# A hybrid encoder layer in fp32: GpSimd takes both halves of the weights that return from DRAM, values stand nine steps behind, linear attention's points are merged

## The chip, the cores and the metric

One core of a Trainium2 chip runs the whole layer. Its engines work side by side, each through its own list of instructions in order, and wait for each other by semaphores: TensorE (PE, matmuls), VectorE (DVE), ScalarE (ACT), GpSimd (POOL) and SyncE (SP), which here only starts DMAs. ScalarE starts DMAs too. The metric is the device time of one execution in microseconds (us); lower is better.

## What is computed

Two sequences of 1024 and 512 tokens of width 1024 go through one layer: RMSNorm, one input projection, three mixers, their gates, the output projection, the residual and a last RMSNorm. Cut to what the change touches:

```python
h = rmsnorm(x, norm_g); z = h @ w_in                      # one projection for all groups
# group A, latent attention, 4 heads
s = einsum(q_nope, k_nope) + einsum(q_rope, k_rope)
p = softmax(s * MLA_SCALE); o = einsum(p, v)
# group C, gated linear attention in chunks of 64, both directions summed
a = einsum('bhid,bhijd,bhjd->bhij', qc, decay, kc)        # inside a chunk
o = o_inter + einsum('bhij,bhje->bhie', a, vc)            # plus the state before the chunk
o = rmsnorm(o_f + o_b, gla_norm_g)
y = rmsnorm(x + concat(gated groups) @ w_out)
```

## The kernel before

The 1536 tokens are 12 tiles of 128 rows. Products that need fp32 are made of three fp32r matmuls: both factors are split into a high part (the value cast to fp32r) and a low part (value minus high), and `product` (L76 to L80) adds high*high, high*low and low*high.

**Front and linear attention.** `phase_front` computes the input projection in 54 blocks of 24 matmuls (128x128 by 512 columns), blocks `i` from 6 on in a plain loop, each in two halves. Between the halves other work is put in. `gla_point(i, half)` numbers the half blocks from block 21 on: p = 0, 1, 2, ... Every tile t of linear attention has three of these points, p = 3t to 3t + 2. At p = 3t TensorE runs `compare(t)`, 56 small matmuls (32 rows by 64 columns) that give all levels of the scores inside the chunks. ScalarE's `copy_top` and VectorE's `choose` (six masked copies, L1076) make the matrix `g_attn` of it. At p = 3t + 2 TensorE runs `turn_rows(t - 2)`, two 128x128 transposes (L1416), and `output(t)`: 16 matmuls of the state (L1398) and 8 of 64x64 with `g_attn` (L1404). ScalarE's `take_rows(t)` fetches the rows and squares them (L681, L685), VectorE's `sum_rows(t)` adds the squares, GpSimd's `invert_rows(t)` takes the inverse root, VectorE's `scale_rows(t)` (L1091) scales the rows in its next tile, and `turn_rows` turns them. `take_outputs` copies four turned tiles at once. ScalarE's list calls this work through `follow(p)`. GpSimd splits the projection's weights (`split_lo`, L805) between these things, in a fixed order.

**Latent attention.** `phase_mla_attend` runs 48 steps m, one per head and tile of queries. The first 8 tiles of a head have 1024 keys, the last 4 have 512. A step: TensorE computes the scores (`scores(m)`, 5 matmuls of 512 columns for every 512 keys); VectorE takes the maximum of a row (`a_top`) and the bias; ScalarE the exponential into `a_weights` (`exponentials`, L1982). In the first three heads (steps 0 to 35) the weights are turned through DRAM: VectorE transposes 32x32 blocks into one of two buffers (`a_weights` slot 2 and `a_spread_second`, L2055), ScalarE starts the store (`store_spread`), and SP, when both tiles of a pair p are stored, starts four loads that bring the pair back turned into `a_turned_lo`, one of three slots (`a_turned_lo`, `_second`, `_third`). ScalarE's `take_high(m)` then casts the loaded values into `a_turned_hi` (L2000), at step m + 5 of its own list, and GpSimd subtracts it in place (L1895). `values(p)` on TensorE (24 or 12 matmuls of 256 columns) needs both. In head 3 TensorE turns the weights itself.

At which step values, the output product (`output(p)`) and the fetch of its result (`gather(p)`) of pair p stand, on all engines, is written in three tuples, `VALUES_AT`, `OUTPUT_AT` and `GATHER_AT`. Before, `values(p)` stood at step 2p + 8 for the first 16 pairs, its output two steps later. Each engine's list is this order written out; there is no scheduler.

## Time and profile before

| | us |
|---|---|
| median of 3 runs | 747.58 |
| the runs | 745.91 to 748.26 |
| the profiled execution, its own time | 750.29 |
| its span in the profile | 748.5 |
| input projection and linear attention | up to 398 |
| latent attention | 398 to 612 |
| output projection, final norm | 612 to 748.5 |

The profile lists for each engine when each instruction started and how long it took. "PE" rows are matmuls and "PEld" rows weight loads. In a timeline the bracket behind a row is the time that the engine stood idle before it and what ended that. The granted clock of TensorE is a share of 2.4 GHz: 1.00 is 2.4, 0.50 is 1.2 GHz.

### The profile page before, as it was taken

How to read it: one execution, taken by the hardware profiler on the slowest of the kernel's cores; microseconds unless marked ns; L12 is line 12 of the kernel's file. 1: busy time of each engine (PE TensorE's matmuls, PEld its weight loads, DVE VectorE, ACT ScalarE, POOL GpSimd, SP SyncE). 2: the span in 40 equal slices, each digit the busy share in tenths (PEclk: the TensorE clock that was granted, in tenths of full speed). 3: DMA queues.
4: the chain of work that ended last, by engine and by line, in shares of the span. 5: the costliest groups of instructions: out<-in, count | busy, mean ns of one | idle time of the engine just before them, and what ended most of it. 6: DMA issues, size and time to landing. Idle time of an engine off the chain costs nothing.

```text
span 748.5 us, 14234 instructions
## 1 busy us (share of the span) xinstructions
PE 721.3 (96%) x5784; PEld 606.4 (81%) x5784; DVE 408.9 (55%) x718; ACT 311.9 (42%) x520; POOL 287.6 (38%) x290
## 2 busy tenths in 40 slices
PE   8999999999999999999999789889989999999996
PEld 6998878878888888888888588788788988888885
DVE  5855877376575543026175757758656654333232
ACT  6554444334423432233223545555554654232321
POOL 3223226366556512122400255553555854322320
PEclk9999999999999999999999889999999999999999
DMA  7613021001122233230235886786886035564441
GB/s 255 183 26 89 28 97 57 30 31 40 63 72 87 73 114 107 92 88 26 63 144 180 249 240 207 230 225 184 264 233 194 1 109 180 176 196 158 139 151 56
DMA packets 65389, 96.14 MB, mean 128 GB/s; under 512 B 6161, under 2 KB 43537, under 8 KB 65330
## 3 DMA queue, kind: packets, MB, share of 16 engines
q1 hardware_dynamic: 53856, 65.34, 30.3%
q10 hardware_dynamic: 11474, 29.96, 10.6%
q8 instruction: 43, 0.70, 0.4%
q14 instruction: 16, 0.13, 0.1%
HBM read 59.30 MB, written 35.00 MB: 126 GB/s over the span
## 4 chain that ended last, share of the span: by engine, by line
PE 76%; DVE 8%; DMA 7%; ACT 4%; POOL 2%; issue 2%; SPq 0%; ACTq 0%; DVEq 0%; POOLq 0%
PE psum L78 20%; PE psum L80 19%; PE psum L79 19%; PE psum L1535 4%; DMA spread_scratch<-a_spread_second 3%; DVE a_top L2082 2%; PE psum L1374 2%; DMA a_turned_lo_third<-spread_scratch 2%; ACT a_weights L1982 2%; POOL a_turned_lo_third L1895 2%; PE psum L1254 1%; DVE g_state L1062 1%; DVE a_weights L2055 1%; DMA a_turned_lo<-spread_scratch 1%; PE psum L1404 1%
## 5 line engine op out<-in xcount | busy, mean ns | idle before, releaser
L78 PE MATMUL psum<-h_hi,z_w_hi 128*128 128x512 f32 x376 | 152.4, 405 | 0.0
L80 PE MATMUL psum<-h_hi,z_w_lo 128*128 128x512 f32 x376 | 146.8, 390 | 0.0
L79 PE MATMUL psum<-h_lo,z_w_hi 128*128 128x512 f32 x376 | 146.6, 390 | 0.0
L78 PEld LDWEIGHTS psum<-h_hi,z_w_hi 128*128 128x128 f32 x376 | 70.6, 188 | 15.9 <-issue 0.7
L80 PEld LDWEIGHTS psum<-h_hi,z_w_lo 128*128 128x128 f32 x376 | 70.6, 188 | 15.4
L79 PEld LDWEIGHTS psum<-h_lo,z_w_hi 128*128 128x128 f32 x376 | 70.7, 188 | 14.0 <-issue 0.7
L1982 ACT ACTIVATE a_weights<-psum,a_bias,mla_q_scale 128x1024 f32<-128x1024 f32 (+1 forms) x48 | 51.0, 1062 | 64.9 <-DVE a_bias L2085 64.9
L805 POOL TENSOR_TENSOR z_w_lo<-z_w_raw,z_w_hi 128x1024 fp32r<-128x1024 f32 x17 | 41.0, 2411 | 94.5 <-ACT z_w_hi L501 92.4
L78 PE MATMUL psum<-o_w_hi,o_m_hi 128*128 128x512 f32 x184 | 72.6, 394 | 0.0
L80 PE MATMUL psum<-o_w_hi,o_m_lo 128*128 128x512 f32 x184 | 72.3, 393 | 0.0
L79 PE MATMUL psum<-o_w_lo,o_m_hi 128*128 128x512 f32 x184 | 72.2, 392 | 0.0
L1895 POOL TENSOR_TENSOR a_turned_lo<-a_turned_lo,a_turned_hi 128x1024 fp32r<-128x1024 f32 x12 | 28.4, 2381 | 73.2 <-ACT a_turned_hi L2000 73.2
L2082 DVE TENSOR_REDUCE a_top<-psum 128x1 f32<-128x1024 f32 (+1 forms) x48 | 49.7, 1035 | 7.5 <-PE psum L2150 7.5
L1076 DVE COPY_PREDICATED g_attn<-g_level_mask,psum 128x256 f32<-128x256 int32 x72 | 32.4, 450 | 38.3 <-ACT g_attn L675 36.2
L2410 DVE TENSOR_TENSOR o_y<-psum,o_x_in 128x512 f32<-128x512 f32 x24 | 16.4, 689 | 53.2 <-PE psum L80 53.2
L514 ACT ACTIVATE z_gate<-psum 128x512 f32<-128x512 f32 x24 | 14.3, 597 | 71.6 <-PE psum L80 71.6
L80 PEld LDWEIGHTS psum<-o_w_hi,o_m_lo 128*128 128x128 f32 x184 | 34.6, 188 | 8.1
L79 PEld LDWEIGHTS psum<-o_w_lo,o_m_hi 128*128 128x128 f32 x184 | 34.6, 188 | 8.0
L78 PEld LDWEIGHTS psum<-o_w_hi,o_m_hi 128*128 128x128 f32 x184 | 34.5, 187 | 7.9
L1895 POOL TENSOR_TENSOR a_turned_lo_third<-a_turned_lo_third,a_turned_hi_third 128x1024 fp32r<-128x1024 f32 (+1 forms) x12 | 22.0, 1846 | 32.3 <-ACT a_turned_hi_third L2000 32.3
L1895 POOL TENSOR_TENSOR a_turned_lo_second<-a_turned_lo_second,a_turned_hi_second 128x1024 fp32r<-128x1024 f32 (+1 forms) x12 | 22.0, 1842 | 27.8 <-ACT a_turned_hi_second L2000 27.8
L2097 DVE TENSOR_TENSOR a_latent_lo<-psum,a_latent_hi 128x256 fp32r<-128x256 f32 x24 | 10.2, 425 | 39.3 <-ACT a_latent_hi L2027 39.3
(281 smaller groups left out, 1656.5 us busy)
## 6 DMA issues: line engine op xcount, KB each, us to landing
z_w_raw<-in_w_z_dram SPq DMA_DIRECT2D x17, 512.0 KB, 3.6
n_x_in<-in_x_dram SPq DMA_DIRECT2D x12, 512.0 KB, 4.3
gates_scratch<-z_gate ACTq DMA_DIRECT2D x24, 256.0 KB, 2.1
spread_scratch<-a_weights ACTq DMA_DIRECT2D x12, 512.0 KB, 5.0
spread_scratch<-a_spread_second ACTq DMA_DIRECT2D x12, 512.0 KB, 6.6
a_turned_lo<-spread_scratch SPq DMA_DIRECT2D x24, 256.0 KB, 5.2
o_x_in<-in_x_dram SPq DMA_DIRECT2D x12, 512.0 KB, 3.6
out_dram<-o_y ACTq DMA_DIRECT2D x11, 512.0 KB, 3.2
```

What stands on the lines that cost most here:

```text
L78: nc.tensor.matmul(out, a_hi, b_hi, start=first, stop=False)
L79: nc.tensor.matmul(out, a_hi, b_lo, start=False, stop=False)
L80: return nc.tensor.matmul(out, a_lo, b_hi, start=False, stop=last)
L514: nc.scalar.activation(stage[:, g % 2, :], bank, ACT.Copy).then_inc(z_emptied, 1)
L805: nc.gpsimd.tensor_tensor(w_lo[:, o % 2, :], raw_of(o)[:, :], w_hi[:, o % 2, :].bitcast(F32), ALU.subtract).then_inc(w_lo_ready, 1)
L1076: nc.vector.copy_predicated(attn[:, t % 2, :, :], level_mask[:, n, :].bitcast(mybir.dt.int32).unsqueeze(1).broadcast_to([P, HEADS, CHUNK]) ...
L1374: mm = nc.tensor.matmul(psum[CHUNK * half:CHUNK * (half + 1), 2 + head, n * CHUNK:(n + 1) * CHUNK], keys, moving, start=True, stop=True, s ...
L1535: mm = nc.tensor.matmul(psum[:, i, part * UNIT:(part + 1) * UNIT], (w_lo if kind == W_LOW else w_hi)[:, o, c], (h_lo if kind == H_LOW else ...
L1895: nc.gpsimd.tensor_tensor(low[:, part], low[:, part].bitcast(F32), high[:, part].bitcast(F32), ALU.subtract)\
L1982: nc.scalar.activation(weights[:, weights_slot(m), 0:count * P].rearrange("p (a k) -> p a k", k=BLK), psum[:, banks, :], ACT.Exp, bias=bia ...
L2082: nc.vector.tensor_reduce(top[:, m:m + 1], psum[:, banks, :], mybir.AxisListType.XY, ALU.max)\
L2410: nc.vector.tensor_tensor(y[:, s, cols], psum[:, 1 - s + 2 * half, :], x_in[:, s, cols], ALU.add)\
```

## The change

Three edits. (1) `take_high` is taken out of ScalarE's list; GpSimd waits for the load itself, casts the tile into the high part and subtracts. (2) The first two values stand at steps 9 and 12, those of pairs 2 to 14 at 2p + 9, pairs 15 and 16 at 38 and 40, the rest as before; the output stands two steps behind for 13 pairs instead of 16. (3) Linear attention has one point per tile, p = 3t: TensorE runs `compare(t)`, then `output(t - 1)`, then `turn_rows(t - 3)`; the other engines follow in that order (`take_rows(t - 1)` before `copy_top(t)`, `sum_rows` and `scale_rows` one tile later). The wait of `compare(t)` for `o_taken` is one tile weaker.

```diff
@@ ACT, follow(p) and what it calls
             def copy_top(t):
                 act.wait_ge(attn_mm, t + 1)
-                if t >= 2:
-                    act.wait_ge(o_mm, t - 1)
+                if t >= 1:
+                    act.wait_ge(o_mm, t)
...
                 if at == 0:
+                    if 1 <= t <= TILES:
+                        take_rows(t - 1)
                     if t < TILES:
                         copy_top(t)
+                    if t % 4 == 2 and 6 <= t < TILES + 3:
+                        take_outputs(t // 4 - 1)
...
                 if at == 2:
-                    if t < TILES:
-                        take_rows(t)
-                    if t % 4 == 1 and 1 < t < TILES + 2:
-                        take_outputs(t // 4 - 1)
@@ DVE, loop over the tiles
-                if t:
-                    scale_rows(t - 1)
-                sum_rows(t)
+                if t >= 2:
+                    scale_rows(t - 2)
+                if t >= 1:
+                    sum_rows(t - 1)
...
+            scale_rows(TILES - 2)
+            sum_rows(TILES - 1)
             scale_rows(TILES - 1)
@@ PE
                     pe.wait_ge(attn_step, STEPS_IN_MASK * t)
-                    pe.wait_ge(o_taken, t)
+                    if t >= 2:
+                        pe.wait_ge(o_taken, t - 1)
...
+                if p >= 0 and p % 3 == 0 and t < TILES + 3:
+                    if t < TILES:
+                        compare(t)
+                    if 1 <= t <= TILES:
+                        output(t - 1)
+                    if t >= 3:
+                        turn_rows(t - 3)
@@ the tuples
-VALUES_AT = tuple(2 * p + 8 for p in range(SPREAD_PAIRS - 2)) + (39, 41, 42, 44, 45, 47, 49, 51)
-LATE_OUTPUTS = SPREAD_PAIRS - 2
+VALUES_AT = (9, 12) + tuple(2 * p + 9 for p in range(2, SPREAD_PAIRS - 3)) + (38, 40, 41, 42, 44, 45, 47, 49, 51)
+LATE_OUTPUTS = SPREAD_PAIRS - 5
@@ POOL, loop over the tiles m of the first three heads
+                if m % 2 == 0:
+                    pool.wait_ge(spread_loaded[m // 2 % 3], 64 * (m // 6) + 64)
+                nc.gpsimd.tensor_copy(high[:, part], low[:, part].bitcast(F32)).then_inc(spread_hi_ready, 1)
                 pool.wait_ge(spread_hi_ready, m + 1)
@@ ACT, loop over the steps
-                if 5 <= m < LAST_HEAD + 5:
-                    take_high(m - 5)
```

TensorE, a tile in the middle of linear attention, before. `h_hi`, `z_w_hi` are the projection; between the two pieces stand 24 of its matmuls:

```order
L80 MATMUL psum<-h_hi,z_w_lo 128x512
L1374 MATMUL psum<-g_q_level_152,g_k_level_153 64x64 [waits g_q_ready,g_k_ready,g_o_taken,g_attn_step]
L1374 MATMUL psum<-g_q_level_152,g_k_level_153 64x64 x47
L1374 MATMUL psum<-z 64x64 x8
L78 MATMUL psum<-h_hi,z_w_hi 128x512 [waits z_emptied,z_w_lo_ready]
```

```order
L80 MATMUL psum<-h_hi,z_w_lo 128x512
L1416 MATMUL psum<-ident,g_o_rows 128x128 [waits g_o_scaled]
L1416 MATMUL psum<-ident,g_o_rows 128x128
L1398 MATMUL psum<-g_state,g_q_ends 64x64 [waits g_ends_ready,g_attn_step]
L1398 MATMUL psum<-g_state,g_q_ends 64x64 x15
L1404 MATMUL psum<-z,g_attn 64x64 x8
L78 MATMUL psum<-h_hi,z_w_hi 128x512 [waits z_emptied,z_w_lo_ready]
```

In the same place after, both pieces have become one (the projection between them now follows without small matmuls in it):

```order
L80 MATMUL psum<-h_hi,z_w_lo 128x512
L1378 MATMUL psum<-g_q_level_152,g_k_level_153 64x64 [waits g_q_ready,g_k_ready,g_o_taken,g_attn_step]
L1378 MATMUL psum<-g_q_level_152,g_k_level_153 64x64 x47
L1378 MATMUL psum<-z 64x64 x8
L1402 MATMUL psum<-g_state,g_q_ends 64x64 [waits g_ends_ready,g_attn_step]
L1402 MATMUL psum<-g_state,g_q_ends 64x64 x15
L1408 MATMUL psum<-z,g_attn 64x64 x8
L1420 MATMUL psum<-ident,g_o_rows 128x128 [waits g_k_taken,g_o_scaled]
L1420 MATMUL psum<-ident,g_o_rows 128x128
L78 MATMUL psum<-h_hi,z_w_hi 128x512 [waits z_emptied,z_w_lo_ready]
```

ScalarE at steps 7 to 9 of head 0, before (`a_spread_second` and `a_weights` with DMA are the stores, `a_turned_hi*` is `take_high`):

```order
L1982 ACTIVATE a_weights,a_total<-psum,a_bias,mla_q_scale 128x1024 [waits a_transposed,a_bias_ready]
L1992 DMA spread_scratch<-a_weights 128x1024 [waits a_spread_loaded0,a_transposed]
L2000 ACTIVATE a_turned_hi_second<-a_turned_lo_second 128x1024 [waits a_spread_loaded1]
L1982 ACTIVATE a_weights,a_total<-psum,a_bias,mla_q_scale 128x512 [waits a_transposed,a_bias_ready]
L1992 DMA spread_scratch<-a_spread_second 128x1024 [waits a_transposed]
L2000 ACTIVATE a_turned_hi_second<-a_turned_lo_second 128x1024 [waits a_spread_loaded1]
L2027 ACTIVATE a_latent_hi<-psum 128x256 [waits a_values_done]
L1982 ACTIVATE a_weights,a_total<-psum,a_bias,mla_q_scale 128x512 [waits a_transposed,a_bias_ready]
L1992 DMA spread_scratch<-a_weights 128x512 [waits a_spread_loaded1,a_transposed]
```

After, with no `take_high` between exponentials and stores, which now follow each other directly:

```order
L1992 ACTIVATE a_weights,a_total<-psum,a_bias,mla_q_scale 128x1024 [waits a_transposed,a_bias_ready]
L2002 DMA spread_scratch<-a_weights 128x1024 [waits a_spread_loaded0,a_transposed]
L1992 ACTIVATE a_weights,a_total<-psum,a_bias,mla_q_scale 128x512 [waits a_transposed,a_bias_ready]
L2002 DMA spread_scratch<-a_spread_second 128x1024 [waits a_transposed]
L1992 ACTIVATE a_weights,a_total<-psum,a_bias,mla_q_scale 128x512 [waits a_transposed,a_bias_ready]
L2002 DMA spread_scratch<-a_weights 128x512 [waits a_spread_loaded1,a_transposed]
L2026 ACTIVATE a_latent_hi<-psum 128x256 [waits a_values_done]
```

GpSimd, pair 0 and the first tile of pair 1, after. Before, the same place held the subtractions alone (L1895), two for each pair, each waiting for `a_spread_hi_ready` from ScalarE; now the wait is for the load:

```order
L1903 CAST a_turned_hi<-a_turned_lo 128x1024 [waits p_rope_stored2,a_spread_loaded0,p_rope_stored1,p_rope_stored0]
L1905 TENSOR_TENSOR a_turned_lo<-a_turned_lo,a_turned_hi 128x1024 [waits a_spread_hi_ready]
L1903 CAST a_turned_hi<-a_turned_lo 128x1024
L1905 TENSOR_TENSOR a_turned_lo<-a_turned_lo,a_turned_hi 128x1024 [waits a_spread_hi_ready]
L1903 CAST a_turned_hi_second<-a_turned_lo_second 128x1024 [waits a_spread_loaded1]
```

GpSimd has taken over what was L2000 in ScalarE's list. TensorE in front of the first values, before and after: the last matmuls of the scores of step 8, and what follows:

```order
L80 MATMUL psum<-mla_ckv_hi,a_q_lo 128x512
L2149 MATMUL psum<-mla_k_rope,a_q_rope 128x512
L2150 MATMUL psum<-mla_k_rope_lo,a_q_rope 128x512
L78 MATMUL psum<-a_turned_hi,mla_tokens_hi 128x256 [waits a_spread_lo_ready,a_turned_lo_ready]
L79 MATMUL psum<-a_turned_lo,mla_tokens_hi 128x256
```

```order
L2148 MATMUL psum<-mla_k_rope,a_q_rope 128x512
L2149 MATMUL psum<-mla_k_rope_lo,a_q_rope 128x512
L78 MATMUL psum<-mla_ckv_hi,a_q_hi 128x512 [waits a_exp_done]
L79 MATMUL psum<-mla_ckv_lo,a_q_hi 128x512
L80 MATMUL psum<-mla_ckv_hi,a_q_lo 128x512
L2148 MATMUL psum<-mla_k_rope,a_q_rope 128x512
L2149 MATMUL psum<-mla_k_rope_lo,a_q_rope 128x512
L78 MATMUL psum<-a_turned_hi,mla_tokens_hi 128x256 [waits a_spread_lo_ready,a_turned_lo_ready]
L79 MATMUL psum<-a_turned_lo,mla_tokens_hi 128x256
```

The scores of step 9, five matmuls with their own wait, have moved in front of the values.

## Rows read from the trace of the kernel before

**Rows 1.** The page's busy times: us (share of the span) x instructions.

```profile
PE 721.3 (96%) x5784; PEld 606.4 (81%) x5784; DVE 408.9 (55%) x718; ACT 311.9 (42%) x520; POOL 287.6 (38%) x290
```

**Rows 2.** Windows: heads 0, 1 and 2 of attention: busy us, clock, DMA share, GB/s.

```profile
398.00:452.00 54.00, 46.40 (x227) 39.76 (x226) 33.70 (x61) 25.94 (x41) 17.19 (x8) 0.91 0.71 204
452.00:503.00 51.00, 46.67 (x267) 40.67 (x266) 36.04 (x71) 27.69 (x45) 25.93 (x13) 0.97 0.79 227
503.00:554.00 51.00, 47.30 (x271) 41.59 (x270) 35.73 (x70) 27.48 (x45) 24.17 (x12) 0.97 0.77 220
```

**Rows 3.** Timeline of TensorE: start us, us, instruction, idle before it and releaser.

```profile
427.72 0.55 PE L78 MATMUL psum<-a_turned_hi,mla_tokens_hi 128*128 128x256 f32 x1 [5.49 <-POOL a_turned_lo L1895]
...
445.54 0.36 PE L78 MATMUL psum<-a_turned_hi_third,mla_tokens_hi 128*128 128x256 f32 x1
...
477.17 0.36 PE L78 MATMUL psum<-a_turned_hi,mla_tokens_hi 128*128 128x256 f32 x1 [1.63 <-POOL a_turned_lo L1895]
...
495.62 0.36 PE L78 MATMUL psum<-a_turned_hi_third,mla_tokens_hi 128*128 128x256 f32 x1 [1.96 <-POOL a_turned_lo_third L1895]
...
546.38 0.36 PE L78 MATMUL psum<-a_turned_hi_third,mla_tokens_hi 128*128 128x256 f32 x1 [1.95 <-POOL a_turned_lo_third L1895]
```

**Rows 4.** A window of head 1 behind a gap; columns as in rows 2.

```profile
496.60:499.90 3.30, 3.30 (x17) 3.30 (x17) 1.28 (x4) 2.93 (x4) 2.52 (x2) 0.50 1.15 279
```

**Rows 5.** Timeline of ScalarE at four of the copies of `take_high`.

```profile
420.90 1.06 ACT L2000 ACTIVATE a_turned_hi<-a_turned_lo 128x1024 fp32r<-128x1024 f32 x1 [0.98 <-DMA a_turned_lo<-spread_scratch]
...
439.49 1.06 ACT L2000 ACTIVATE a_turned_hi_third<-a_turned_lo_third 128x1024 fp32r<-128x1024 f32 x1 [3.17 <-DMA a_turned_lo_third<-spread_scratch]
...
470.95 1.06 ACT L2000 ACTIVATE a_turned_hi<-a_turned_lo 128x1024 fp32r<-128x1024 f32 x1 [0.39 <-DVE a_weights L2055]
...
489.61 1.06 ACT L2000 ACTIVATE a_turned_hi_third<-a_turned_lo_third 128x1024 fp32r<-128x1024 f32 x1 [1.66 <-DMA a_turned_lo_third<-spread_scratch]
```

**Rows 6.** Timeline of SP's queue, the four loads of pair 6; the page's landing.

```profile
460.37 1.80 SPq L1863 DMA_DIRECT2D a_turned_lo<-spread_scratch  x4
...
a_turned_lo<-spread_scratch SPq DMA_DIRECT2D x24, 256.0 KB, 5.2
```

**Rows 7.** Groups of GpSimd's instructions by form: busy us, mean ns, idle before.

```profile
L1895 POOL TENSOR_TENSOR a_turned_lo<-a_turned_lo,a_turned_hi 128x1024 fp32r<-128x1024 f32 x12 | 28.4, 2381 | 73.2 <-ACT a_turned_hi L2000 73.2
...
L798 POOL TENSOR_TENSOR n_rstd<-n_rstd,n_minus_half 128x1 f32<-128x1 f32 x12 | 7.5, 624 | 0.9
...
L1921 POOL CAST o_w_hi<-o_w_raw 128x512 fp32r<-128x512 f32 x8 | 4.7, 619 | 0.0
...
L863 POOL COPY z_window_sums<-z 128x1024 f32<-128x1024 f32 x2 | 2.1, 1044 | 0.0
```

**Rows 8.** Timeline of VectorE: a transpose that waited for a store.

```profile
480.62 1.25 DVE L2055 STREAM_TRANSPOSE a_spread_second<-a_weights 128x1024 f32<-128x1024 f32 x1 [1.11 <-DMA spread_scratch<-a_spread_second]
```

**Rows 9.** Timeline of TensorE around a comparison of linear attention.

```profile
237.31 0.39 PE L80 MATMUL psum<-h_hi,z_w_lo 128*128 128x512 f32 x1
237.63 1.19 PE L1374 MATMUL psum<-g_q_level,g_k_level 32*64 32x64 f32 x92
...
238.68 0.41 PE L1374 MATMUL psum<-z 32*64 32x64 f32 x13
239.02 0.50 PE L78 MATMUL psum<-h_hi,z_w_hi 128*128 128x512 f32 x1
239.36 0.39 PE L79 MATMUL psum<-h_lo,z_w_hi 128*128 128x512 f32 x1
```

**Rows 10.** Timeline of VectorE behind the same comparison: masked copies, scaling.

```profile
239.54 2.88 DVE L1076 COPY_PREDICATED g_attn<-g_level_mask,psum 128x256 f32<-128x256 int32 x6 [3.25 <-ACT g_attn L675]
...
246.01 0.42 DVE L1091 TENSOR_TENSOR g_o_rows<-g_o_rows,g_stats 128x256 f32<-128x256 f32 x1
```

**Rows 11.** Timeline of VectorE: one op beside GpSimd's subtraction, one alone.

```profile
79.05 3.92 DVE L985 TENSOR_TENSOR z_window_sums<-z_window_sums 128x1567 f32<-128x1567 f32 x1 [1.93 <-POOL z_window_sums L863]
83.00 1.79 DVE L987 TENSOR_TENSOR z_window_sums<-z_window_sums 128x1566 f32<-128x1566 f32 x1
```

18 lines of the change are left out of this document (3 added, 15 removed).

## The prediction

> **What bounds the kernel now.** I read the page's busy times first, then the windows by stage, then every gap of TensorE, then what each gap waited for. TensorE is busy 721.3 of 748.5 us [rows 1], so time comes only from its idle time, its clock, or cheaper matmuls. From 57 to 398 us, projection and linear attention, it has no idle time to speak of; there only the matmuls' own cost can change. The four heads of latent attention are 398 to 612 us, one head a window, the first three shown [rows 2]: idle are 54 - 46.40 = 7.6 us in head 0, 51 - 46.67 = 4.3 in head 1, 51 - 47.30 = 3.7 in head 2; head 3 hardly has any. The gaps end at the first matmul of `values(p)`, and their releaser is GpSimd's L1895, the low part [rows 3]. The output stage behind it (612 us on) runs on TensorE at full load and is not touched. After such gaps the granted clock is at the lower of its two levels (1.2 instead of 2.4 GHz) for about 3.3 us, once each in heads 1 and 2, and for some 10 us in all in head 0 (54 x 0.09 x 2; [rows 2]); one stretch stands as a row [rows 4]. It came behind the gap of 1.96 us at 495.62 and the like one of head 2, not behind the 1.63 us at 477.17.
>
> What GpSimd waits for is the copy `take_high` on ScalarE, and there two things are mixed. At 420.90, 439.49 and 489.61 ScalarE itself stands idle for the load (up to 3.17 us), with the next exponential queued behind [rows 5]: a wait for a transfer becomes a wait of exponentials, transposes and stores, hence of the next transfers. At 470.95 the data is long there: the load's four issues run 460.37 to 462.2 and land 5.2 us later [rows 6], at about 467.4, and only the step in which the copy stands in ScalarE's order makes it wait 3.5 us more.
>
> **Part 1: GpSimd takes high and low.** A 128x1024 low part costs 2.38 us; a copy of that size on GpSimd 1.04 us, and the cast from f32 to fp32r, the form that is added, 0.62 us for 512 elements, half of it and a little [rows 7]. I take 1.05 us, ScalarE's own 1.06 [rows 5]. A pair of 1024-key tiles is then ready 2 x (1.05 + 2.38) = 6.9 us after its load has landed. Sum over the phase: 24 x 3.43 + 12 x 1.92 = 105 us of GpSimd in some 145 us; per pair 6.9 us against about 8.4 us that a pair of steps takes TensorE, so it keeps up, with 1.5 us to spare. ScalarE loses 36 copies (24 x 1.06 + 12 x 0.63 = 33 us), none of it on the path by itself, and its stops for loads, which are.
>
> What this is worth depends on the pair. Pair 0 (step 8): landed by 420.9, ready at 427.8, exactly where it is now (427.72): nothing gained by GpSimd. Pair 6: landed 467.4, ready 474.3 instead of just before 477.17, and TensorE asks at 475.5: the gap goes. Pair 8: landed 489.6, ready 496.5, where it started at 495.62; here GpSimd alone would be 0.9 us worse, since the copy of the second half no longer runs beside the first half's subtraction.
>
> **Part 2: values nine steps behind.** TensorE's total work is the same; more scores stand ahead of each `values`. In front of pair 0 stood the scores up to step 8, now those of step 9 too, a short step (512 keys, 5 x 0.227 = 1.13 us). So the 5.49 us become about 4.4. Pair 2 moves from step 12 to step 13, a long step of 10 x 0.227 = 2.27 us. It landed 439.5 [rows 5], so is ready at 446.4, where it started at 445.54 [rows 3]: TensorE starts it 0.9 us later but with 2.27 us more done, a net 1.4 us. That is the whole gain of head 0 up to there (the 1.1 us of pair 0 are in it), so two gaps of about 4 and 3 us, and both slow-clock stretches, stay. Heads 1 and 2: pair 8 is asked for at 493.66 + 2.27 = 495.9 against 496.5, a rest of 0.6. TensorE is then also some 3.7 us ahead (1.4 of head 0, 1.63 and 0.6 of pairs 6 and 7), which the loads follow only in part, as the stores wait for each other: DVE stands 1.11 us before a transpose until the store of two tiles earlier has left its buffer [rows 8]. I put 0.8 us back per head (bounds 0, and 3.7 where the loads follow not at all). Gain of the two: 4.3 + 3.7 - 1.5 = 6.5 us. Pairs 15 to 17, asked for in head 3, move by at most a step: 0.
>
> Clock: with gaps below 1.6 us in heads 1 and 2 their two stretches of 3.3 us at half rate go, 1.7 us each: 3.3 us (bounds 0 and 7, all four).
>
> **Part 3: linear attention's points merged.** Per tile TensorE now leaves the 128x128 matmuls twice (comparison; turn and output), then once. Price of leaving and coming back [rows 9]: the matmuls of 512 columns start every 0.227 us. The comparison should start at 237.54 and starts at 237.63. Its 112 records go by at (238.68 - 237.63) / 99 = 10.6 ns, so they would be through at 238.73; the second large matmul behind them starts at 239.36, where without a loss it would be at 238.96. Loss 0.40 us, in and out together. Twelve comparisons and twelve outputs make 24 places; 13 remain, 11 go. Inside a merged point comparison and output have the same shape and need no new switch. 11 x 0.35 = 3.9 us (starts and ends in this view are modelled, so a little off the 0.40; bounds 0 and 4.4). This stage has no cover, so all of it counts.
>
> What is moved and what it could cost: ScalarE's `take_rows` and `copy_top` now stand behind the output, so DVE's masked copies, which start 1.9 us behind the comparison (239.54 [rows 10]), start about 2.3 us later: the rest of the point, 1.1 us, and two passes of some 0.4 us, and a semaphore or two. `scale_rows` ran 8.4 us behind the comparison (246.01), so comes at 10.7; the transposes that read it stand in the next point, 10.9 + 2.4 = 13.3 us behind: 2.6 us to spare. GpSimd's `invert_rows` in front of the w_lo split waits longer, up to a point's length; the split has two points (22 us) until TensorE needs it. SP's queue is passed by the store of the outputs half a block later (2.7 us), its data wanted 100 us on. I put all this at 0.
>
> **Sum.** Head 0 1.4, heads 1 and 2 6.5, clock 3.3, points 3.9: 15.1 us. The profiled execution took 750.29 us with a span of 748.5, 2.7 us above the median of 747.58, within the runs' own spread; the difference is taken from the median: 732.5 us.
>
> **A rule against part 1.** The DVE op with two inputs from SBUF that ran beside a GpSimd subtraction took 3.92 us, the same op alone 1.79 [rows 11]: it lost about the time of the subtraction. In the attention phase DVE's transposes and reductions read one tensor or PSUM, and the transpose at 480.62, which has a subtraction of GpSimd (2.4 us) beside it from 480.7 on, took 1.25 us [rows 8]. So I price contention at 0. The Trainium skill says the same in "GPSIMD Engine Reference", Key points: the two share SBUF interfaces and contend when DVE has two SBUF inputs or is in a two-port mode. Were the transposes such instructions, its rule would slow them or the copy; by it the forecast would turn into the third rival below; the trace speaks against it.
>
> **Rivals.**
> A. The gaps only move. Stores and loads set the pace (DMA busy 0.77 to 0.79 of heads 1 and 2 [rows 2]; the DVE wait [rows 8]), so TensorE meets the same transfers one step later. For it: pair 0 and pair 2 above. Against: at 470.95 it was the order, not the transfer. Then each head gets its 3.7 us back at one pair, clock falls included: what stays is 3.9 + 1.4 + (8.0 - 7.4) = 5.9, 741.7 us.
> B. The switch is not worth anything, or output and transposes inside a point lose as much: 732.5 + 3.9 = 736.4 us.
> C. Slower: GpSimd becomes the bound. If the cast beside running loads costs what the subtraction does, 2.38 us, a large pair takes 9.5 us and a small one 5.2, and each of a head's 12 subtractions pauses some 0.08 us for the cast in front of it (0.9 us over 12 such pairs of ops, L798 in [rows 7]): a head takes 4 x 9.5 + 2 x 5.2 + 0.9 = 49.3 us, against the 51 - 4.3 - 1.7 = 45.0 us of work that TensorE has in head 1. Three heads x 4.3 = 12.9 us, which holds the gaps not gained, 2.7 more at pair 0, and the clock's 3.3 not gained: 732.5 + 18.9 = 751.4 us. It decides from about 1.8 us a cast, where a large pair needs the 8.4 us that its steps take; slower than before from about 2.2 us. Against: the rows are at 1.04 and 2 x 0.62, and the subtraction keeps its 2.38 over 12 instances with all kinds of work beside them.
>
> **Chances.** Forecast 0.67, A 0.17, B 0.09, C 0.07. Range 727 to 742: the low end has 5.5 us less (the rest of the clock and of the gaps in head 0 partly gone), the high end takes in A and B; C is left out. A measurement of this kernel tells about 0.3%, 2.2 us, from no change. Faster 0.90, the same 0.03, slower 0.07.
>
> **What would show it.** Part 1: GpSimd casts of 1.05 us, ScalarE's waits for loads gone, L1895's successor no longer waiting for ScalarE. Part 2: gaps in front of pairs 6, 7, 12, 13 gone, those of pairs 0 and 2 at 3 to 4.5 us; clock 1.00 in the windows of heads 1 and 2. Part 3: 132 us of linear attention shorter by about 3.9, matmul counts equal. Wrong if the cast takes over 1.5 us, if gaps of 2 us stand at pairs 8 and 14, or if the transposes in linear attention wait for DVE.

## The result and the profile after

| | us |
|---|---|
| changed kernel, median of 6 runs | 741.93 (738.69 to 744.05) |
| before, median of 6 runs beside them | 747.92 (745.91 to 748.37) |
| ratio | 0.9913, 95% interval 0.9888 to 0.9937 |
| the changed kernel again, 6 runs, with 17 of before | 741.30 against 749.27, 0.9889 (0.9857 to 0.9921) |
| profiled execution, its own time and its span | 744.05, 741.8 |

It is faster by 6.0 us, where 15.1 were forecast; with the second comparison 6 to 8. The profiled execution is the longest of its six.

The page of the changed kernel, busy times, answers [rows 1]. TensorE lost 5.0 us of busy time, its share is 97%:

```profile
PE 716.3 (97%) x5784; PEld 605.1 (82%) x5784; DVE 398.9 (54%) x718; ACT 282.8 (38%) x484; POOL 315.5 (43%) x326
```

To see where the 6.7 us between the spans (748.5 to 741.8) come from, cut both traces where TensorE has done the same work: at the first matmul of the attention phase (its query projection; the stage table above rounds this border to 398), at the last scores of step 20, at those of step 38 (the same values and outputs lie behind them in both kernels), and at the first matmul of the output product. Columns are length, busy time of PE, PEld, DVE, ACT and POOL, then granted clock, DMA share and GB/s. Before:

```profile
394.25:474.02 79.77, 72.01 (x368) 61.58 (x367) 52.79 (x93) 40.13 (x64) 26.02 (x13) 0.94 0.72 212
474.02:555.96 81.94, 74.02 (x420) 64.80 (x419) 54.91 (x110) 43.34 (x72) 41.27 (x20) 0.96 0.81 228
555.96:614.41 58.45, 57.01 (x394) 51.85 (x393) 38.45 (x83) 34.97 (x68) 36.92 (x36) 1.00 0.34 107
```

After:

```profile
391.53:473.74 82.21, 73.99 (x367) 62.84 (x366) 54.96 (x96) 29.62 (x51) 41.29 (x28) 0.92 0.74 216
473.74:547.35 73.61, 70.48 (x419) 61.75 (x417) 52.76 (x108) 27.68 (x54) 52.74 (x36) 1.00 0.84 235
547.35:607.74 60.39, 56.93 (x393) 52.03 (x393) 38.40 (x83) 32.34 (x62) 41.34 (x41) 1.00 0.37 114
```

Attention begins 394.25 - 391.53 = 2.7 us earlier. The first stretch is 2.4 us longer than before, the second 8.3 shorter, the third 1.9 longer: 2.7 - 2.4 + 8.3 - 1.9 = 6.7. Length less PE gives idle time: 7.8 to 8.2, 7.9 to 3.1, 1.4 to 3.5. The rest is the clock: at 1.00 the second stretch is 70.5 us of work instead of 74.0, while the first needs 74.0 instead of 72.0 at a granted clock of 0.92 instead of 0.94: TensorE ran longer at 1.2 GHz.

The gaps of TensorE that are left, in its timeline (bracket: idle before, and what ended it); they answer [rows 3]:

```profile
425.08 0.55 PE L78 MATMUL psum<-a_turned_hi,mla_tokens_hi 128*128 128x256 f32 x1 [3.54 <-POOL a_turned_lo L1905]
444.15 0.55 PE L78 MATMUL psum<-a_turned_hi_third,mla_tokens_hi 128*128 128x256 f32 x1 [3.40 <-POOL a_turned_lo_third L1905]
455.83 0.39 PE L78 MATMUL psum<-a_turned_hi,mla_tokens_hi 128*128 128x256 f32 x1 [0.68 <-DVE mla_mixed L2063]
486.12 0.38 PE L78 MATMUL psum<-a_turned_hi_second,mla_tokens_hi 128*128 128x256 f32 x1 [1.24 <-DVE mla_mixed L2063]
532.25 0.39 PE L78 MATMUL psum<-a_turned_hi_second,mla_tokens_hi 128*128 128x256 f32 x1 [0.91 <-DVE mla_mixed L2063]
539.29 0.41 PE L2185 MATMUL psum<-ident,a_share 128*128 128x128 f32 x2 [0.98 <-DVE a_latent_lo L2096]
549.71 0.36 PE L78 MATMUL psum<-a_turned_hi,mla_tokens_hi 128*128 128x256 f32 x1 [2.20 <-POOL a_turned_lo L1905]
```

Pairs 0 and 2 still wait for GpSimd; pairs 6 to 8 and 12 to 14 no longer do. New in these heads are waits for VectorE: for `gather` (L2063), which frees the bank of PSUM that `values` writes, and for `a_latent_lo`. New is also the wait of 2.20 us for GpSimd in front of pair 15, which had no gap. Before, the wait for `gather` had one row, in front of pair 17 in head 3, on the weight load of that matmul:

```profile
572.93 0.19 PEld L78 LDWEIGHTS psum<-a_turned_hi_third,mla_tokens_hi 128*128 128x128 f32 x1 [0.97 <-DVE mla_mixed L2064]
```

GpSimd does what was forecast: a cast of 1.04 us begins when the load has landed, and pair 0 is ready 425.08 - 418.01 = 7.1 us later.

```profile
418.01 1.04 POOL L1903 CAST a_turned_hi<-a_turned_lo 128x1024 fp32r<-128x1024 f32 x1 [53.71 <-DMA a_turned_lo<-spread_scratch]
419.13 2.39 POOL L1905 TENSOR_TENSOR a_turned_lo<-a_turned_lo,a_turned_hi 128x1024 fp32r<-128x1024 f32 x1
421.47 1.04 POOL L1903 CAST a_turned_hi<-a_turned_lo 128x1024 fp32r<-128x1024 f32 x1
422.58 2.35 POOL L1905 TENSOR_TENSOR a_turned_lo<-a_turned_lo,a_turned_hi 128x1024 fp32r<-128x1024 f32 x1
```

For the matmul at 486.12 VectorE's timeline shows the chain of the new waits: a transpose that waits 1.54 us for the store of two tiles earlier, behind it two query subtractions, `a_latent_lo`, and only then the gather:

```profile
478.67 1.25 DVE L2054 STREAM_TRANSPOSE a_spread_second<-a_weights 128x1024 f32<-128x1024 f32 x1 [1.54 <-DMA spread_scratch<-a_spread_second]
...
484.26 0.69 DVE L2046 TENSOR_TENSOR a_q_lo<-psum,a_q_hi 128x512 fp32r<-128x512 f32 x1 [1.05 <-ACT a_q_hi L1977]
484.87 0.41 DVE L2096 TENSOR_TENSOR a_latent_lo<-psum,a_latent_hi 128x256 fp32r<-128x256 f32 x1
485.20 0.41 DVE L2061 COPY a_share_row<-psum 128x256 f32<-128x256 f32 x1
485.65 0.42 DVE L2063 TENSOR_TENSOR mla_mixed<-psum,a_share_row 128x256 f32<-128x256 f32 x1
```

In linear attention one gap has come that was not there:

```profile
204.95 0.38 PE L1420 MATMUL psum<-ident,g_o_rows 128*128 128x128 f32 x2 [1.16 <-issue]
```

"issue" says that the profile shows nothing that TensorE waited for. From 57 us to the start of attention TensorE's busy time fell by 4.0 us (336.7 to 332.7) and its idle time grew by 1.3 (0.6 to 1.8). Without this stall the stage would have given 3.9 us.

### The profile page after: what moved, and what is told of

Read it like the earlier page. It is cut to its first block, busy times and chain, and to the rows that moved or that the text cites. A ratio compares the mean times of both kernels' runs of the same rounds, so it can differ in the third digit from the quotient of the medians.

```text
span 741.8 us, 14234 instructions
## 1 busy us (share of the span) xinstructions
PE 716.3 (97%) x5784; PEld 605.1 (82%) x5784; DVE 398.9 (54%) x718; ACT 282.8 (38%) x484; POOL 315.5 (43%) x326
## 4 chain that ended last, share of the span: by engine, by line
PE 77%; DVE 8%; DMA 7%; ACT 3%; POOL 2%; issue 2%; SPq 0%; ACTq 0%; DVEq 0%; POOLq 0%
PE psum L78 20%; PE psum L79 20%; PE psum L80 20%; PE psum L1540 4%; DMA spread_scratch<-a_spread_second 4%; PE psum L1378 2%; DVE a_top L2081 2%; PE psum L1257 1%; DVE g_state L1062 1%; DMA a_turned_lo_third<-spread_scratch 1%; DVE a_spread_second L2054 1%; PE psum L1408 1%; DMA a_turned_lo<-spread_scratch 1%; ACT a_weights L1992 1%; PE psum L1433 1%
## 5 line engine op out<-in xcount | busy, mean ns | idle before, releaser
L78 PE MATMUL psum<-h_hi,z_w_hi 128*128 128x512 f32 x376 | 150.8, 401 | 0.0
L1903 POOL CAST a_turned_hi<-a_turned_lo 128x1024 fp32r<-128x1024 f32 x12 | 12.5, 1039 | 67.8 <-DMA a_turned_lo<-spread_scratch 67.7
L839 POOL TENSOR_TENSOR g_stats<-g_stats,n_minus_half 128x4 f32<-128x4 f32 x12 | 12.1, 1008 | 58.4 <-DVE g_stats L1086 58.4
L78 PE MATMUL psum<-mla_ckv_hi,a_q_hi 128*128 128x512 f32 x80 | 31.9, 398 | 0.6 <-ACT a_weights L1992 0.6
L79 PE MATMUL psum<-mla_ckv_lo,a_q_hi 128*128 128x512 f32 x80 | 31.5, 394 | 0.0
```

What stands on the lines that cost most here:

```text
L78: nc.tensor.matmul(out, a_hi, b_hi, start=first, stop=False)
L79: nc.tensor.matmul(out, a_hi, b_lo, start=False, stop=False)
L1903: nc.gpsimd.tensor_copy(high[:, part], low[:, part].bitcast(F32)).then_inc(spread_hi_ready, 1)
```

## Experiments: the three parts one by one

**e1, the points alone.** The edit is the change's hunks in `follow`, VectorE's tile loop, `compare` and the points, nothing of attention.

> The kernel before with linear attention's points merged and nothing else. In the traces the stage up to the latent attention is 2.7 us shorter with the merged points, and it holds one stall of TensorE of 1.17 us (at 204.95, in front of the first turn of rows) that the kernel before has not. Theory 1 (the parts of the change add up, this stage is independent of the rest): 2.7 us, so 0.9964 of before, and the same stall in the same place; 3.9 us and 0.9948 if the stall belongs to that one execution only. Rival (what is gained in front is lost at the first loads of latent attention, which the store of the rope parts opens at its own time): under 1 us, 0.999 or more.

Measured: 746.14 (12 runs) against 747.66 (29), 0.9978 (0.9957 to 1.0000). The trace has attention start at 391.67, 2.6 us earlier, and the stall in the same place:

```profile
205.13 0.38 PE L1420 MATMUL psum<-ident,g_o_rows 128*128 128x128 f32 x2 [1.26 <-issue]
```

The interval holds 0.9964 and also 0.999, where the rival begins, and leaves 0.9948 just outside. So the times do not decide between 2.7 us and the rival. That the stage itself is 2.6 to 2.7 us shorter is read from the traces, and e4 below, the change without its points, gains 3.3 us where the whole change gains 6 to 8. The stall is the change's.

**e2, GpSimd takes high and low, values where they were.**

```diff
+                if m % 2 == 0:
+                    pool.wait_ge(spread_loaded[m // 2 % 3], 64 * (m // 6) + 64)
+                nc.gpsimd.tensor_copy(high[:, part], low[:, part].bitcast(F32)).then_inc(spread_hi_ready, 1)
...
-                if 5 <= m < LAST_HEAD + 5:
-                    take_high(m - 5)
```

> The kernel before with GpSimd taking high and low parts, values where they were. Theory 1 (my forecast's working, part 1 alone): gaps of pairs 6, 7, 12 and 13 go, 1.63 + 0.62 + 1.29 + 0.45 = 4.0 us, the gaps of pairs 8 and 14 grow by 0.9 each, head 0's stay; the low clock behind pairs 8 and 14 stays. Net 2.2 us: 745.7, ratio 0.997. Rival (the loads, and not the order of ScalarE's list, set the pace: TensorE meets the same transfers a little later): the gaps gained at pairs 6 and 7 come back at 8, ratio 0.999 to 1.001.

Measured: 750.85 (12 runs), 1.0025 (1.0003 to 1.0048). Both theories fell: it is slower. The gaps of pairs 6 and 12 went, as expected. Those of pairs 7 and 13 did not: they are 0.96 and 1.05 us (0.63 and 0.45 before). And those of pairs 1, 8 and 14 grew by 1.4 to 1.6 us each (2.11, 1.96 and 1.95 before):

```profile
438.24 0.58 PE L78 MATMUL psum<-a_turned_hi_second,mla_tokens_hi 128*128 128x256 f32 x1 [3.46 <-POOL a_turned_lo_second L1900]
497.40 0.55 PE L78 MATMUL psum<-a_turned_hi_third,mla_tokens_hi 128*128 128x256 f32 x1 [3.48 <-POOL a_turned_lo_third L1900]
550.40 0.36 PE L78 MATMUL psum<-a_turned_hi_third,mla_tokens_hi 128*128 128x256 f32 x1 [3.55 <-POOL a_turned_lo_third L1900]
```

Pair 8 had landed at 490.30 (first cast in GpSimd's timeline, behind a wait for the load), and 7.1 us later it was ready. By these rows, where the load is late, the copy on ScalarE beside the subtraction was worth more than the freedom of its list.

**e3, the values later, the copy still on ScalarE.** `LATE_OUTPUTS` changes with it, as in the change.

```diff
-VALUES_AT = tuple(2 * p + 8 for p in range(SPREAD_PAIRS - 2)) + (39, 41, 42, 44, 45, 47, 49, 51)
+VALUES_AT = (9, 12) + tuple(2 * p + 9 for p in range(2, SPREAD_PAIRS - 3)) + (38, 40, 41, 42, 44, 45, 47, 49, 51)
```

> The kernel before with the values one step later and the copy still in ScalarE's list, five steps behind its tile. Theory 1 (the two parts need each other: the copy stands in ScalarE's list, and when TensorE is ahead ScalarE waits there for the load with the next exponential behind it): gaps at the values of heads 1 and 2 fall to under 1 us each, but ScalarE's waits for loads (9.8 us of idle time by such rows in the trace before) grow and TensorE waits for exponentials instead; gain at most 2 us, ratio 0.997 to 1.003. Rival (the place of the values does it all and GpSimd's copy is not needed): heads 1 and 2 gain the 8 us that the changed kernel gained there, ratio 0.990.

Measured: 756.51 (6 runs), 1.0109 (1.0086 to 1.0131), slower than either theory had it. The longest of its waits has the mechanism of the first, with another victim: not the exponential but the copy of a latent result stands behind ScalarE's wait for a load. In heads 1 and 2 TensorE waits for `gather` four more times, 0.98 to 2.41 us. ScalarE's timeline, and TensorE's output behind it:

```profile
440.24 1.06 ACT L2000 ACTIVATE a_turned_hi_third<-a_turned_lo_third 128x1024 fp32r<-128x1024 f32 x1 [5.05 <-DMA a_turned_lo_third<-spread_scratch]
441.21 0.37 ACT L2027 ACTIVATE a_latent_hi<-psum 128x256 fp32r<-128x256 f32 x1
```

```profile
442.18 0.66 PE L2186 MATMUL psum<-ident,a_share 128*128 128x128 f32 x2 [7.22 <-DVE a_latent_lo L2097]
```

**e4, both together without the points.**

> The changed kernel with linear attention's points as before: parts 1 and 2 together. Theory 1 (parts add): 2.7 us slower than the changed kernel, so 3.3 us faster than before, ratio 0.9956; head 0 of latent attention not shorter than before, heads 1 and 2 shorter by 8 us, and 1.9 us lost again in head 3 in front of pair 15. Rival (merging the points shifted the load times against TensorE and made head 0's second stretch of low clock longer): head 0 here as short as forecast, 1.4 us shorter than before, and the ratio 0.992.

Measured: 744.33 (12 runs), 0.9959 (0.9939 to 0.9979), the ratio of theory 1. Alone the two parts cost 3.2 and 8.9 us, together they give 3.3: each pays only with the other. Steps 20 to 38 take 75.0 us here (81.9 before) and the last stretch 59.55 (58.45). The first stretch is 78.9 us, 0.9 shorter than before, a length between the two theories. But of it 70.8 is busy time, so 8.1 us are idle, not less than before (7.8); only less of it ran at the lower clock (0.98):

```profile
394.26:473.15 78.89, 70.81 (x367) 59.57 (x366) 55.04 (x96) 29.62 (x51) 41.33 (x28) 0.98 0.76 224
```

So head 0's gaps are no shorter without the points either, and the points are not what cost its gain.

## Experiments: where the forecast gain went

**The changed kernel again.**

> The changed kernel again, as it is, beside the next ones on the same chip. Its six runs so far lie between 738.69 and 744.05, and the profiled one is the longest of them, at a mean clock of 0.990 where the shortest had 0.994. Theory 1 (part of what is missing from the forecast is which pauses happen to be followed by the lower clock, and that differs from run to run): a median of 740 to 743, again with runs 3 us apart, and in the new profile the stretches of low clock behind other gaps than in the first, with the gaps themselves alike. Rival (the low clock belongs to the kernel): both long stretches in head 0 again, 6.8 us each.

Measured: 741.30 (6 runs). The gaps are alike (3.42 and 3.68 us in front of pairs 0 and 2, 1.49 of pair 15), the clock is not: the stretch up to step 20 has 72.6 us of busy time at 0.96, not 74.0 at 0.92.

```profile
391.39:472.70 81.31, 72.61 (x367) 61.07 (x366) 54.84 (x96) 29.56 (x51) 41.34 (x28) 0.96 0.73 219
```

Twelve runs of this kernel lie between 738.69 (mean clock 0.994) and 744.05 (0.990). The 61 runs of before from three comparisons go with their mean clock too (correlation -0.74, about 0.6 us for 0.001), from 0.9905 on average to 0.9927 for the twelve: 1.3 us, as an estimate from this slope. Theory 1 stands in the median and in the spread, not in the place: the low clock came behind the same two gaps as in the first trace, but for 3.4 us each instead of 6.8. The rival is out.

**e5, output and gather earlier.** On TensorE `output(p)` goes in front of `values(p + 1)`, on VectorE `gather(p)` in front of the next `a_latent_lo`, for p < 13:

```diff
@@ DVE
+                for p in pair_at(m, OUTPUT_AT):
+                    if p < GATHER_FIRST:
+                        gather(p)
                 for p in pair_at(m, VALUES_AT):
                     dve.wait_ge(latent_hi_ready, p + 1)
@@ PE
+                for p in pair_at(m, OUTPUT_AT):
+                    if p < GATHER_FIRST:
+                        output(p)
                 for p in pair_at(m, VALUES_AT):
                     values(p)
```

> The changed kernel with output(p) put in front of values(p + 1) in TensorE's step and gather(p) right behind it on VectorE, instead of at the head of the next step, for the first 13 pairs. In the changed kernel TensorE waits three times in heads 0 to 2 for such a gather at the first matmul of a values: 0.67 at 455.83, 1.23 at 486.12, 0.91 at 532.25. Theory 1 (this wait is a new one, made by the odd step at which values now stand, with the transposes of VectorE in front of the gather): the three gaps go, 2.8 us less than the changed kernel, ratio to before 0.9875. Rival (the load of the next pair is right behind): the gaps move to the low part on GpSimd at the following values, under 1 us.

Measured: 739.75 (6 runs), 0.9870 (0.9837 to 0.9902); against 741.30 1.5 us, which these few runs hardly tell from none. The three gaps went, but not to GpSimd: the output, now earlier, waits for `a_latent_lo`, 1.00 and 1.61 us where it had not, and 0.66 us where it had waited 0.98. VectorE was late itself, whatever stood last in its list. Neither theory named that.

**e6, pair 15 one step later.** `VALUES_AT` with 39 for 38.

> The changed kernel with pair 15 at step 39 instead of 38. My forecast put nothing on pair 15, whose step did not move. In the profile TensorE, some 8 us ahead there, waits 2.20 us for its low part (549.71). Theory 1 (all steps in front gained a step of cover and this one did not): step 39 adds 2.27 us of scores and a turn in front of it, the gap goes, 1.9 to 2.2 us less than the changed kernel. Rival (pair 16 at 40 and the slot that pair 15 frees late are next): TensorE waits at pair 16 or 17 instead, under 0.7 us gained.

Measured: 745.14 (12 runs), 0.9950 (0.9927 to 0.9974), 3.8 us slower than the changed kernel beside it. The gap went from pair 15, and three came in its place: 1.50 and 0.64 us at the turns of head 3's weights, and 2.08 us at pair 17, which waits for the gather of pair 15. The step behind pair 15's place in head 3 is not free, as the rival said.

**e12, half the bytes.** From pair 6 on stores and loads move half. The kernel leaves out the other half of these weights, whose places keep older values, so it is a measurement and no kernel to use. The store's edit:

```diff
-                act.dma_start(spread_dram[count][p % 3, m % 2], spread[m % 2][:, 0:count]).then_inc(spread_stored[m % 2], 16)
+                part = count // 2 if p >= 6 else count
+                act.dma_start(spread_dram[count][p % 3, m % 2][:, 0:part], spread[m % 2][:, 0:part])\
+                   .then_inc(spread_stored[m % 2], 16)
```

> The changed kernel with half the bytes in the stores and loads of the weights from pair 6 on (heads 1 and 2): each store writes the first half of a tile's columns, each load brings four of eight blocks; the rest of the buffers keeps older values. It asks what sets the gaps left in heads 1 and 2 and in front of pair 15. Theory 1 (the transfers: VectorE waits 1.54 and 1.22 us for a store before a transpose, with the query's subtraction and the gather queued behind it; pair 15 follows its load by GpSimd's 6.9 us): gaps of 0.67, 1.23, 0.91, 0.99 and 2.20 fall to 0.5 in all from pair 6 on, 4.5 us less than the changed kernel: 737. Rival (the order of work on VectorE and ScalarE at the three steps in which the next head's queries are projected): the gaps at 486.12, 532.25 and 539.29 stay, only pair 15's goes: 739.5.

Measured: 736.16 (4 runs), 0.9844 (0.9821 to 0.9866), 5.3 us below 741.5, the median of the changed kernel's twelve runs. The same three stretches of its trace:

```profile
391.54:471.20 79.66, 72.86 (x367) 62.09 (x366) 55.04 (x96) 29.59 (x51) 43.09 (x30) 0.94 0.66 201
471.20:541.05 69.85, 69.85 (x421) 62.28 (x420) 52.56 (x108) 27.81 (x54) 56.97 (x39) 1.00 0.41 127
541.05:598.96 57.91, 56.66 (x394) 51.88 (x392) 38.40 (x83) 32.38 (x62) 35.64 (x36) 1.00 0.36 112
```

From step 20 to 38 TensorE has no gap left (69.85 of 69.85), and pair 15 has none. Against the repeat's trace these two stretches are together 5.5 us shorter. So what is left in heads 1 and 2, the gathers too, comes from the transfers: VectorE is late because it waits for stores. Order on VectorE alone, the rival, is out. In head 0, whose bytes are all there, pair 2's gap was 1.99 us in this trace, so that gap differs by over 1 us from one execution to the next.

**e8, each cast twice.** A second `tensor_copy` with its own semaphore in front of the first.

> The changed kernel with every cast on GpSimd done twice, 1.12 us more for a tile of 1024 keys with the pause between (rows of the changed kernel: cast 1.04, next instruction 1.12 behind it), 2.2 more for a pair. It asks at how many pairs GpSimd's time stands bare behind the load, which my forecast put at pairs 0 and 2 and, by 0.6 us, at pair 8 and its like. Theory 1: pairs 0 and 2 of head 0, pairs 8 and 14 (pair 8 ready at 494.1, asked for at 494.2: nothing to spare) and pair 15 each 2.2 us later; GpSimd waits 3.4 us for the load of each pair, so nothing adds up from pair to pair. 11 us and the low clock behind two more gaps: 750 to 754. Rival (in heads 1 and 2 GpSimd is covered as forecast and TensorE's gaps there come from VectorE): only head 0, 4.4 us: 745.5 to 746.5.

Measured: 752.58 (8 runs), 1.0064 (1.0042 to 1.0086), 11 us more than the changed kernel. GpSimd's time stands bare behind the load at pairs 0 (5.76 us now), 8 (2.49), 14 (1.31) and 15 (3.66), and at pair 13 (0.78); pair 2's gap grew by 0.3 only, since TensorE came 2.2 us later itself. In attention TensorE is idle 6.9 us longer than in the changed kernel's trace and busy 2.7 longer, at a clock of 0.95 instead of 0.97: the casts account for part of the time, the lower clock for the rest. Theory 1 stands for where GpSimd is bare: in heads 1 and 2 the last pair of 1024 keys has no slack.

**e10, ScalarE helps at three pairs.**

```diff
+CAST_BY_SCALAR = {1: (7, 1), 5: (12, 2), 31: (37, 3)}
@@ POOL
+                if m in CAST_BY_SCALAR:
+                    pool.wait_ge(cast_helped, CAST_BY_SCALAR[m][1])
+                    nc.gpsimd.tensor_tensor(low[:, part], low[:, part].bitcast(F32), high[:, part].bitcast(F32), ALU.subtract)\
+                      .then_inc(spread_lo_ready, 1)
+                    continue
@@ ACT, in front of exponentials(m)
+                for tile, (step, _) in CAST_BY_SCALAR.items():
+                    if m == step:
+                        cast_high(tile)
```

> The changed kernel with ScalarE casting the second tile of pairs 0, 2 and 15 while GpSimd subtracts in the first, at moments when ScalarE stands idle in the profile (before the exponentials of steps 7, 12 and 37). A pair is then ready 1.1 us earlier behind its load. Theory 1 (the gaps at these three pairs are load plus GpSimd, nothing else): 3.53, 3.39 and 2.20 each become 1.1 less, 3.3 us in all, 1 us of it given back where the next load is waited for: 739 us, ratio to the changed kernel 0.997. Rival (ScalarE's stop for the load delays an exponential and so a store, the next load follows): gaps move, within 1 us of the changed kernel.

Measured: 738.89 (7 runs), 0.9894 (0.9873 to 0.9915). In the trace, which is of the shortest of the seven, pair 15's gap is 0.41, pair 2's 1.64 (1.99 to 3.68 in traces without the help), pair 0's only 0.4 smaller:

```profile
424.50 0.50 PE L78 MATMUL psum<-a_turned_hi,mla_tokens_hi 128*128 128x256 f32 x1 [3.17 <-POOL a_turned_lo L1907]
441.76 0.36 PE L78 MATMUL psum<-a_turned_hi_third,mla_tokens_hi 128*128 128x256 f32 x1 [1.64 <-POOL a_turned_lo_third L1907]
```

**e11, help and gather together.**

> The last kernel together with the earlier output and gather of the first 13 pairs. Alone the earlier gather was 1.5 us faster than the changed kernel (739.75 against 741.3). Theory 1 (they stand at different places): 1.5 + 2.3 us, 737.5. Rival (both only bring TensorE to the same transfers earlier): 739 to 740.

Measured: 736.66 (6 runs), 0.9858 (0.9833 to 0.9882). Nearer to the sum (737.5) than to the rival (739 to 740).

**e13, pair 0's cast a step earlier.** `{1: (6, 1), ...}` in e11.

> The kernel with the help of ScalarE and the earlier gather, with the cast for pair 0 one step earlier in ScalarE's list. In the run with the help ScalarE began this cast at 420.88, behind the store of tile 6 and a copy of the queries, 3.1 us after the load had landed (417.76), and GpSimd waited 0.73 us for it; the gap at pair 0 fell from 3.53 to 3.17 only. Theory 1 (this gap is load plus GpSimd): the cast begins at about 418, GpSimd does not wait, pair 0 is ready 0.7 us earlier, gap 2.5 us; the next exponential comes up to 0.6 later, which nobody waits for: 736 us. Rival (the exponential later means a store later, which the second and third load wait for): pair 2's gap grows by as much, 736.7 or more.

Measured: 735.83 (5 runs), 0.9834 (0.9808 to 0.9860), not to be told from e11, the lowest median of a kernel that computes all. Pair 0 gained what theory 1 said (a gap of 2.27 us), and pair 2's grew from 1.31 in e11 to 1.99, with 1.14 us in front of the first output: in this pair of traces what the first gap gave, the next two took, as the rival said. The median fits theory 1's 736 as well, and pair 2's gap varies by as much by itself, so the runs do not decide.

**e14, no rotary load beside the store.** The kernel leaves out one block's load and its wait; that block of head 1 computes with head 0's rotary queries.

> The changed kernel without the load of the rotary queries of head 1, block 0 (four transfers of 64 KB behind the load of pair 1; that block of head 1 keeps head 0's values). In the changed kernel the store of tile 5, issued at 420.27, lands at about 427.4, 7.1 us where 3.2 is the median, with the load of pair 1 (418.96) and these four (420.90) beside it; pair 2's load waits for it. Theory 1 (transfers set head 0's second gap): the store lands 0.8 us earlier (256 KB at the 320 GB/s of such stretches), so does pair 2, and its gap falls from 3.4 to about 2.6; the whole kernel at most 0.8 us faster, which a comparison can't tell from none. Rival (the store waits for what stands in front of it in its own queue): no row of head 0 moves.

Measured: 740.82 (4 runs), 0.9891 (0.9861 to 0.9922). The store of tile 5 lands 6.7 us after its issue instead of 7.1, pair 2 is ready 0.6 us earlier, its gap is 3.11 instead of 3.40. That is less than the gap varies by itself: with head 0 as in the changed kernel it was 3.68, 2.67 and 1.99 us in the traces of the repeat, e6 and e12, and pair 2's cast began at 435.84 in e12, earlier than here (436.52). So the direction is theory 1's, and the size is not shown. Head 0's own stores and loads were not halved; its second gap stays explained by pair 2's late load, not taken apart further.

**e9, the turn in front.**

```diff
+                    if t >= 3:
+                        turn_rows(t - 3)
                     if t < TILES:
                         compare(t)
                     if 1 <= t <= TILES:
                         output(t - 1)
-                    if t >= 3:
-                        turn_rows(t - 3)
```

> The changed kernel with the turn of the rows in front of the comparison inside the point, not behind the output. It asks what the stall of 1.17 us (204.95, no releaser) is, which stands in front of the first turn. Theory 1 (TensorE's instructions do not arrive fast enough: the point holds some 320 matmul and weight instructions within 2.5 us, and an instruction load begins 202.5, inside it): the stall stays, about 1.2 us, at nearly the same number of instructions, so now in front of the projection's matmul behind the point. Rival (the turn waits for scaled rows or for a bank of PSUM that the profile does not show): the stall moves with the turn, in front of the comparison, or is gone.

Measured in one run: 744.54, with a wait of 1.9 us at 95.92 in a stage that the edit does not touch. The first turn has no gap now; the stall stands in the middle of the outputs, and a second one in another tile:

```profile
206.95 0.27 PE L1408 MATMUL psum<-z,g_attn 64*64 64x64 f32 x2 [0.85 <-issue]
229.64 0.32 PE L1402 MATMUL psum<-g_state,g_q_ends 32*64 32x64 f32 x2 [1.12 <-issue]
```

Both lie inside a row of equal matmuls whose waits are long behind. That speaks against the rival: no wait for data stands there. It is not quite theory 1's place either, which was the projection's matmul behind the point. What is left is that TensorE's instructions had not come; the section on the hardware has the rows for it.

## Why the prediction was wrong, point by point

Of the 15.1 us some 8.5 are missing. Head 0 lacks 3.9 of them (its gaps and its clock) and head 3 1.9, two places that the sum had as a sure gain and as nothing; heads 1 and 2 lack 1.5 and the points 1.2.

**Part 1, the times on GpSimd: right.** Cast 1.04 (forecast 1.05), pair 0 ready 7.1 us behind the load (6.9), GpSimd itself not the bound: rival C did not come. But "pair 8 0.9 us worse" by GpSimd alone was 1.5 (e2), and pair 1, whose 2.11 us are within the 7.6 of head 0 [rows 2], was not priced at all; in e2 they became 3.46.

**Part 2, head 0: wrong.** The two gaps were well foreseen, 4.4 and about 3 against 3.54 (with 0.55 a little ahead of it, for an exponential) and 3.40. The step that failed is the bookkeeping behind them: "a net 1.4 us. That is the whole gain of head 0". By the prediction's own figures the gaps left were 4.4 + 3 = 7.4 us, those of before 7.6 [rows 2], so there was no 1.4 of idle time to have; pair 2 started 52.6 us after attention began, where it had been 51.3, so 1.3 later and not 0.9, and 0.68 us at a gather came on top. Idle time up to step 20 went from 7.8 to 8.2 (8.7 in the repeat).

**Part 2, heads 1 and 2: mechanism right, size off.** Idle time fell from 7.9 to 3.1 us, 4.8 instead of 6.5. The term that failed is "I put 0.8 us back per head": it was 1.7 us too small over the two heads. It asked how far the loads follow, and looked for the answer in front of `values`; it came back through VectorE, whose transposes wait for stores, and with them the gather that `values(p + 2)` waits for. In heads 0 to 2 that semaphore had no row in the trace before, its one row lay in head 3 (572.93), and the prediction did not ask what else `values` waits for. e12 shows it: with half the bytes these gaps are 0.

**Part 2, head 3: wrong.** "Pairs 15 to 17 move by at most a step: 0." Pair 15 did not move at all, and that is the loss: everything ahead of it had become 8 us faster, its load only 5.7. SyncE's queue, before and after:

```profile
539.56 3.01 SPq L1863 DMA_DIRECT2D a_turned_lo<-spread_scratch  x4
```

```profile
533.87 1.80 SPq L1868 DMA_DIRECT2D a_turned_lo<-spread_scratch  x4
```

The stretch became 1.2 us longer in the repeat's trace and 1.9 in the first.

**Clock: right in heads 1 and 2, and a part that was not asked.** Their busy time fell by 3.5 us (forecast 3.3) at a granted clock of 1.00. In head 0 the lower clock behind the two gaps took 2.0 us more than before in the profiled run, 0.6 in the repeat and 1.2 less in e4, with gaps alike. Over all runs the mean clock rose by 0.0022, worth 1.3 us. The forecast took head 0's share as fixed, which was the other half of its loss there.

**Part 3, the points: the price of the switch was right, the stall was missed.** 3.9 us forecast, 2.7 come, and 1.2 is the stall at the second point that holds all three pieces. The prediction had weighed what the move could cost on VectorE, GpSimd and SyncE ("I put all this at 0") and did not ask what TensorE's own list of instructions costs when it is this dense. VectorE's slack held, no transpose waited. Rival B is out.

The sum: 15.1 less 1.2 (stall), 1.9 (head 0's gaps, 1.4 + 0.5), 2.0 (its clock), 1.5 (heads 1 and 2, 1.7 too little idle time and 0.2 more clock), 1.9 (head 3) is 6.6, and the traces differ by 6.7.

**Rival A** gave 741.7 us, nearly the measured time, but by luck, since its sum is another: it let heads 1 and 2 give their gain and the clock back, where they kept 8.3 us, and it kept head 0's 1.4 with its clock as it was, gave the points 3.9 and left pair 15 alone, which together are about as much the other way. Its mechanism, transfers that set the pace once the order no longer does, is what e12 found; I gave it 0.17, though the DMA share of 0.77 to 0.79 [rows 2] and VectorE's wait for a store [rows 8] both spoke for it.

## What to carry to other kernels

When a stage gets faster, go through every entry of its schedule that did not move and ask what stands there when all before it comes early; "unmoved" is not 0. Read a step's whole list of waits, not only the one that ends last today: two edits that each cost 3 and 9 us alone gave 3 together, and the next wait was a semaphore that had one row before, in another head. And whether order or transfers set the rest was settled here by one run with half the bytes. Last, a change of a gap by 0.3 us in one trace says little where the same gap differs by over 1 us between traces of the same code.

## What the runs showed of the hardware

**Instructions can come late for TensorE.** In the changed kernel's DMA view of 202 to 203 us (40 slices of 25 ns), one packet of the instruction queue moves in slice 20, at 202.5 us, and the stall ends at 204.95:

```profile
DMA  0000000000000000000900000000000000000000
...
q8 instruction: 1, 0.02, 6.9%
```

In e9 such a packet lies at 204.8, and the stall ends at 206.95, 2.15 us behind. For its second stall, which ends at 229.64, the packet lies at 227.4 (view of 227 to 229 us, slices of 50 ns):

```profile
DMA  0000000900000000000000000000000000000000
```

In all eleven traces with the change's own order in the points the stall is there, 0.8 to 1.4 us long, and ends 2.2 to 2.5 us behind such a packet. The merged point has 162 matmul records and as many of weight loads within 2.4 us. Such packets also come where nothing stalls (in the kernel before at 202.6 us, 1.3 us ahead of the comparison), and other points have as many records and run without a stall. The point before, at 190.47, is the first with all three pieces, and the stall is always in the second. So what decides seems to be where the packet falls in the stream; this was not tried further. That the packet carries TensorE's instructions, and that TensorE waits for them, is read from this pattern and from e9, not seen directly. The Trainium skill ("Runtime: NRT & Kernel Launch", Instruction fetch mechanics) has blocks of 16 KiB fetched on a DMA queue of the engine's own, and the fetch hidden by the time an instruction takes to issue; the packet's 0.02 MB agree, and if the reading above is right, the hiding does not hold here.

**The same gaps, another clock.** With gaps of 3.1 to 3.7 us in front of pairs 0 and 2, TensorE's busy time up to step 20 was 74.0, 72.6 and 70.8 us in three traces (changed kernel, its repeat, e4), at clocks of 0.92, 0.96 and 0.98. By windows of 0.5 us the lower clock (1.2 GHz) of pair 0's gap lasted about 6.8, 3.4 and 3.4 us in the three, that of pair 2's gap 6.8, 3.4 and nothing at all, though that gap was 3.14 us. In the kernel before a gap of 1.96 us, at 495.62, had been enough for 3.3 us of it [rows 4]. What a gap costs beyond its own length is not a constant of the kernel; a profile of one execution can be off by it by 1 to 2 us on either side, as these three are.
